# Eight recurrent heads: decay operands through PSUM, a reordered second turn, and a value tile in two column halves

## The reference, cut to what matters

```python
b = jnp.cumsum(logf, axis=2)
diff = b[:, :, :, None, :] - b[:, :, None, :, :]
decay = jnp.exp(jnp.minimum(diff, 0.0)) * causal
attn = jnp.einsum('bhtd,bhsd,bhtsd->bhts', q, k, decay)
o = (jnp.einsum('bhts,bhsv->bhtv', attn, v)
     + jnp.einsum('bhtd,bhdv->bhtv', q * jnp.exp(b), S))
b_last = b[:, :, -1:, :]
k_dec = k * jnp.exp(b_last - b)
S_new = (jnp.exp(b_last[:, :, 0, :])[..., None] * S
         + jnp.einsum('bhsd,bhsv->bhdv', k_dec, v))
```

## Time and profile before

| | |
|---|---|
| median of 3 runs | 852.73 us (850.11 to 853.77) |
| profiled execution | 853.36 us, its span 851.1 us |
| TensorE products busy | 811.1 us, 95% |
| VectorE / ScalarE / GpSimd busy | 405.9 / 233.0 / 141.5 us |
| head turns | about 21 to 170 us of the span |
| mean granted TensorE clock | 0.990 |

### The profile page before, as it was taken

One profiled execution on the slowest core, in us unless ns is written; L12 is line 12 of the kernel. 1 busy time (PEld: TensorE's weight loads), 2 busy tenths in 40 slices (PEclk: granted clock), 3 DMA queues, 4 the chain that ended last, 5 costly groups with the idle time before them and its releaser, 6 DMA issues.

```text
span 851.1 us, 12448 instructions
## 1 busy us (share of the span) xinstructions
PE 811.1 (95%) x5068; PEld 525.1 (62%) x5068; DVE 405.9 (48%) x682; ACT 233.0 (27%) x373; POOL 141.5 (17%) x170
## 2 busy tenths in 40 slices
PE   4999999999999999999999999999999999998892
PEld 2989999999999977585353533535335353352251
DVE  6789999988999723875011212112021120210127
ACT  6666655665444360111102010010000100000011
POOL 1354555433777200000000000000000000000000
PEclk9999999999999999999999999999999999999996
DMA  8422222344446453669999999999999999999971
GB/s 319 169 85 85 85 85 85 109 179 156 149 151 240 205 198 149 267 239 389 432 394 424 428 427 424 428 428 425 427 427 428 424 429 427 428 424 429 428 325 64
DMA packets 33894, 251.33 MB, mean 295 GB/s; under 512 B 4974, under 2 KB 8430, under 8 KB 21674
## 3 DMA queue, kind: packets, MB, share of 16 engines
q1 hardware_dynamic: 31296, 249.18, 71.8%
q10 hardware_dynamic: 2538, 1.32, 0.5%
HBM read 247.99 MB, written 2.48 MB: 294 GB/s over the span
## 4 chain that ended last, share of the span: by engine, by line
PE 69%; DVE 11%; DMA 9%; ACT 8%; issue 1%; ACTq 1%; DVEq 0%
PE ps L543 67%; DMA ring<-in_w_up_e 8%; DVE ring L1692 4%; ACT ring L1212 2%; ACT ar L1222 1%; DVE ar L1728 1%; ACT split_w L1131 1%; DVE ar L1739 1%; PE ps L940 1%; DVE ar L1683 1%; ACTq L1261 1%; ACT ar L1184 1%; DVE ring L1601 1%; DVE ar L1735 1%; ACT ar L1183 0%
## 5 line engine op out<-in xcount | busy, mean ns | idle before, releaser
L543 PE MATMUL ps<-ring,ar 128*64 128x512 f32 (+1 forms) x976 | 202.1, 567 | 1.6 <-DMA ring<-in_w_up_e 1.2
L543 PE MATMUL ps<-ring,xT 128*64 128x512 f32 (+2 forms) x848 | 151.0, 455 | 6.1 <-DMA ring<-in_w_gate_e 3.1
L543 PEld LDWEIGHTS ps<-ring,ar 128*64 128x64 f32 x976 | 67.9, 137 | 121.1 <-issue 111.8
L543 PEld LDWEIGHTS ps<-ring,xT 128*64 128x64 f32 (+1 forms) x848 | 75.5, 154 | 74.3 <-issue 63.8
L543 PE MATMUL ps<-split_x,split_t 128*128 128x320 f32 x672 | 99.2, 309 | 0.0
L543 PEld LDWEIGHTS ps<-split_x,split_t 128*128 128x128 f32 x672 | 98.6, 188 | 0.2
L2105 DVE TENSOR_TENSOR ar<-ar,ps 128x512 f32<-128x512 f32 (+1 forms) x42 | 28.7, 684 | 135.0 <-PE ps L543 134.3
L543 PE MATMUL ps<-split_x,split_w 128*128 128x320 f32 x480 | 79.8, 322 | 3.8 <-DVE split_w L1652 1.2
L543 PEld LDWEIGHTS ps<-split_x,split_w 128*128 128x128 f32 x480 | 73.2, 193 | 7.0 <-ACT split_x L1166 2.1
L1815 DVE SCALAR_TENSOR_TENSOR ps<-ar,params,ps 128x350 f32<-128x350 f32 x116 | 68.1, 587 | 4.1
L543 PE MATMUL ps<-ar 128*64 128x512 f32 (+7 forms) x424 | 66.8, 342 | 0.0
(11 more groups left out here) (232 smaller groups left out, 850.3 us busy)
## 6 DMA issues: line engine op xcount, KB each, us to landing
ring<-in_w_gate_e SPq DMA_DIRECT2D x29, 2048.0 KB, 21.8
ring<-in_w_up_e SPq DMA_DIRECT2D x29, 2048.0 KB, 18.6
ring<-in_w_down_e SPq DMA_DIRECT2D x22, 2048.0 KB, 18.1
ring<-in_w_in SPq DMA_DIRECT2D x56, 512.0 KB, 4.5
ar<-in_w_down_e SPq DMA_DIRECT2D x4, 1792.0 KB, 18.9
ring<-in_w_down_end SPq DMA_DIRECT2D x3, 2048.0 KB, 36.7
ar<-in_w_up_e SPq DMA_DIRECT2D x3, 1792.0 KB, 14.8
ring<-in_w_o_a SPq DMA_DIRECT2D x8, 512.0 KB, 5.8
```

The source lines that it names most:

```text
L543: return pe.matmul(out, lhsT, rhs, start=start, stop=stop)
```

## The change

- **VectorE's decays.** After the scan ScalarE's new `sum_copy` copies `hb` into PSUM bank 0 (signal `b_ps`). `level_decay` waits for it and takes its first operand there; the second, the broadcast end of the half, stays in SBUF. `cur_f` now waits for `dr_ready` (level_decay done).
- **Query sides.** `query_side` and the q product of `carry_side` read bank 1 instead of `hq`. The factor 128^-0.5 moves into the query weights (`w_high` and `w_low`). `cur_q` now waits for `qeb_ready` of the previous head.
- **Second turn.** On TensorE `levels` and `prev_kT` come ahead of `cur_q`. In the tail `levels(3, 1)` move ahead of the 16 small products into bank 1 and of `rms(3, 0)`.
- **V's third tile.** Its eight products alternate by k between output partitions 0 to 63 and 64 to 127, so that two partial sums arise. The key side of that tile is doubled to match (`hkde` has 384 columns, `levels` forms the third tile for both halves), and `prev_kT`, `prev_states` and `prev_out` use all 128 partitions, whose sum joins the two. The copies of V and kT on ScalarE become one instruction each; GpSimd's last add of `level_sums` becomes two.

```diff
             def cur_f(i, b, first):
-                    pe.wait_ge(h["ls_ready"], 2 * i + b)
+                    pe.wait_ge(h["dr_ready"], 2 * i + b)
             def cur_q(i, b, first):
-                    pe.wait_ge(h["q_sb"], 2 * i + b)
+                    pe.wait_ge(h["qeb_ready"], 2 * i + b)
             def value_tile(b, t):
                 for k in range(KT):
-                    last = mm(ps[0:n, 3, t * P:t * P + P], xT[:, k, t0:t0 + n], sh[:, b, 3, k, :], k == 0, k == KT - 1)
+                    if t < 2:
+                        last = mm(ps[0:n, 3, t * P:t * P + P], xT[:, k, t0:t0 + n], sh[:, b, 3, k, :], k == 0, k == KT - 1)
+                    else:
+                        side = slice(k % 2 * BLK, k % 2 * BLK + BLK)
+                        last = mm(ps[side, 3, t * P:t * P + P], xT[:, k, t0:t0 + n], sh[:, b, 3, k, :], k < 2, k >= KT - 2)
             def levels(i, b, first):
-                        for m in range(n // BLK):
-                            s0 = t0 + BLK * m
+                        for m in range(2):
+                            s0 = t0 + BLK * m * (t < 2)
             def prev_kT(i, b, first):
-                    last = pe.transpose(ps[0:n, 7, t * P:t * P + P], hkde[:, t0:t0 + n], ident)
+                    last = pe.transpose(ps[:, 7, t * P:t * P + P], hkde[:, t * P:t * P + P], ident)
             def prev_states(i, b):
-                    last = mm(ps[:, 7, t * P:t * P + P], hkT[0:n, t, :], hV[0:n, t, :], True, True)
+                    last = mm(ps[:, 7, t * P:t * P + P], hkT[:, t, :], hV[:, t, :], True, True)
             def prev_out(i, b, first):
-                mm(ps[:, 6, 256:320], hV[0:64, 2, :], hAS[0:64, 2, 0:64], False, True).then_inc(h["o_done"], 1)
+                mm(ps[:, 6, 256:320], hV[:, 2, :], hAS[:, 2, 0:BLK], False, True).then_inc(h["o_done"], 1)
             def head_turn(cur, prev, pprev, first=False, first_prev=False):
-                if first or first_prev:
+                if first:
                     cur_q(*cur, first)
                 if first_prev:
+                    levels(*prev, True)
                     prev_kT(*prev, True)
-                    levels(*prev, True)
+                    cur_q(*cur, first)
                     prev_states(*prev)
...
-            pe.wait_ge(h["ls_ready"], 8)
+            pe.wait_ge(h["dr_ready"], 8)
             conv_value(0)
-            pe.wait_ge(h["q_sb"], 8)
+            levels(3, 1, False)
+            pe.wait_ge(h["qeb_ready"], 8)
             for k in range(KT):
                 mm(ps[:, 1, T:T + 2 * NE], ones, wgb[:, k, :], k == 0, k == KT - 1)
             rms(3, 0, 1)
-            levels(3, 1, False)
             prev_kT(3, 1, False)
...
+            def sum_copy(i, b):
+
+                n = 2 * i + b
+                act.wait_ge(h["b_ready"], n + 1)
+                signal(act, act.activation(ps[:, 0, 0:T], hb, ACT.Copy), h["b_ps"], n + 1)
...
                 key_exp(*cur)
+                if first_prev:
+                    sum_copy(*cur)
                 if prev:
                     prev_states(*prev, first_prev)
+                if not first_prev:
+                    sum_copy(*cur)
...
             def level_sums(i, b, first):
-                signal(pool, pool.tensor_tensor(hAS[0:BLK, :, 0:BLK], hAM[0:BLK, :, 0:BLK], hAM[0:BLK, :, BLK:2 * BLK], ALU.add), h["as_ready"], 2 * n + 2)
+                signal(pool, pool.tensor_tensor(hAS[0:BLK, 0:2, 0:BLK], hAM[0:BLK, 0:2, 0:BLK], hAM[0:BLK, 0:2, BLK:2 * BLK], ALU.add), h["as_ready"], 2 * n + 1)
+                signal(pool, pool.tensor_tensor(hAS[:, 2, 0:BLK], hAM[:, 2, 0:BLK], hAM[:, 2, BLK:2 * BLK], ALU.add), h["as_ready"], 2 * n + 2)
...
             def level_decay(i, b):
+                dve.wait_ge(h["b_ps"], n + 1)
-                    ins = dve.tensor_tensor(xv[:, :, hs:2 * hs], bv[:, :, hs:2 * hs], bv[:, :, hs - 1:hs].to_broadcast([P, w // (2 * hs), hs]), ALU.subtract)
+                    here = ps[:, 0, 0:w].rearrange("p (m s) -> p m s", s=2 * hs)[:, :, hs:2 * hs]
+                    ins = dve.tensor_tensor(xv[:, :, hs:2 * hs], here, bv[:, :, hs - 1:hs].to_broadcast([P, w // (2 * hs), hs]), ALU.subtract)
             def query_side(i, b):
-                    qv = hq[:, b, 0:w].rearrange("p (m s) -> p m s", s=2 * hs)[:, :, hs:2 * hs]
-                    ins = dve.tensor_tensor(xv, xv, qv, ALU.mult)
+                    qv = ps[:, 1, 0:w].rearrange("p (m s) -> p m s", s=2 * hs)[:, :, hs:2 * hs]
+                    ins = dve.tensor_tensor(xv, qv, xv, ALU.mult)
             def carry_side(i, b, first):
-                signal(dve, dve.tensor_tensor(hqeb, heb, hq[:, b, :], ALU.mult), h["qeb_ready"], n + 1)
-                signal(dve, dve.tensor_tensor(hkde, hkde, hk[:, b, :], ALU.mult), h["kdec_ready"], n + 1)
+                signal(dve, dve.tensor_tensor(hqeb, ps[:, 1, 0:T], heb, ALU.mult), h["qeb_ready"], n + 1)
+                cc(dve.tensor_tensor(hkde[:, 0:SEQ], hkde[:, 0:SEQ], hk[:, b, 0:SEQ], ALU.mult))
+                both_sides = hkde[:, SEQ:SEQ + P].rearrange("p (s n) -> p s n", s=2)
+                key_twice = hk[:, b, SEQ:T].rearrange("p (o n) -> p o n", o=1).to_broadcast([P, 2, BLK])
+                signal(dve, dve.tensor_tensor(both_sides, both_sides, key_twice, ALU.mult), h["kdec_ready"], n + 1)
```

More of the change, by code:

```diff
@@ L630, in prev_kT @@
                     pe.wait_ge(h["so_ready"], 2 * i + b)
-                for t, (t0, n) in enumerate(TILES):
-                    last = pe.transpose(ps[0:n, 7, t * P:t * P + P], hkde[:, t0:t0 + n], ident)
+                for t in range(3):
+                    last = pe.transpose(ps[:, 7, t * P:t * P + P], hkde[:, t * P:t * P + P], ident)
                 last.then_inc(h["kT_done"], 1)
@@ L1130, in w_high @@
                     act.wait_ge(h[("f_done", "q_done")[q]], n)
-                signal(act, act.activation(piece(wh, q), sh[:, b, q].rearrange("p k n -> p (k n)"), ACT.Copy), whi_ready, 2 * n + q + 1)
+                signal(act, act.activation(piece(wh, q), sh[:, b, q].rearrange("p k n -> p (k n)"), ACT.Copy, scale=(1.0, QSCALE)[q]), whi_ready, 2 * n + q + 1)
             def u_high(c, q):
@@ L1221, in tile_exp @@
                 for t, (t0, c) in enumerate(TILES):
[L1222 to L1223 removed]
+                    dst, src = hkde[:, t0:t0 + c], hb[:, t0:t0 + c]
+                    if t == 2:
+                        dst = hkde[:, SEQ:SEQ + P].rearrange("p (s n) -> p s n", s=2)
+                        src = src.rearrange("p (o n) -> p o n", o=1).to_broadcast([P, 2, BLK])
+                    signal(act, act.activation(dst, src, ACT.Exp, scale=-1.0, bias=hb[:, t0 + c - 1:t0 + c]), h["kde_ready"], 3 * n + t + 1)
             def prev_states(i, b, first):
@@ L1651, in w_low @@
                 dve.wait_ge(whi_ready, 2 * n + q + 1)
-                signal(dve, dve.tensor_tensor(piece(wl, q), sh[:, b, q].rearrange("p k n -> p (k n)"), piece(whF, q), ALU.subtract), wlo_ready, 2 * n + q + 1)
+                raw = sh[:, b, q].rearrange("p k n -> p (k n)")
+                ins = dve.scalar_tensor_tensor(piece(wl, q), raw, QSCALE, piece(whF, q), ALU.mult, ALU.subtract) if q else dve.tensor_tensor(piece(wl, q), raw, piece(whF, q), ALU.subtract)
+                signal(dve, ins, wlo_ready, 2 * n + q + 1)
             def u_low(c, q):
@@ L1734, in last_mask @@
                     dve.wait_ge(h["as_ready"], 2 * n)
-                signal(dve, dve.tensor_tensor(hAM[0:BLK, 2, :], ps[0:BLK, LEVEL_BANKS[2], 0:LW], mask[0:BLK, :], ALU.mult), h["am_ready"], 2 * n + 2)
+                signal(dve, dve.tensor_tensor(hAM[:, 2, :], ps[:, LEVEL_BANKS[2], 0:LW], mask, ALU.mult), h["am_ready"], 2 * n + 2)
             def level_fold(i, b):
```

25 lines of the change are left out of this document (9 added, 16 removed).

## The result

The changed kernel takes 842.67 us (median of 5 runs, 841.39 to 844.99); the kernel before takes 850.81 (median of 5 runs: the three of the forecast's base and two more). The ratio is 0.9908 with a 95% interval of 0.9892 to 0.9923, that is 7.8 us off, where 5.8 were forecast. The predicted 847.0 and its range from 844.6 both lie above this, 1.9 us of it because the base itself went from 852.73 to 850.81. The direction and the circle that sets the new turn are as forecast; sizes were missed.

What follows compares the result with a forecast made beforehand. The start of TensorE's piece behind the eight head turns was taken to bound the kernel. -4.8 to rms of turn 7 and -0.8 after gave -5.6 (floor -6.3); -5.8 was taken: 847.0 us, range 844.6 to 851.0.

Steps and rivals of the forecast that it cites:

- rms of turn 2: TensorE after turn 1's new order and its hole: rms at 59.2 against 59.05, a loss of 0.15 us.
- What bounds the kernel: TensorE's piece from 181 to 367 us: its start moves its end, and the weight stream behind starts earlier by as much.
- The first circle: VectorE and ScalarE waiting on each other set the 19.24 us turn; with the change it becomes 17.6.
- level_decay: VectorE's seven instructions in a steady turn fall from 4.15 to 2.5 us with one operand in PSUM.
- sum_copy: ScalarE's new copy costs nothing in steady turns; in turn 0 level_decay starts 0.6 us later and ends 0.3 sooner.
- V's third tile: TensorE's eight products overlap in four pairs, saving 0.94 of V's 5.66 us a turn.
- K=128 instead of 64 does not change a product's columns: nothing: TensorE's third-tile products over 128 rows instead of 64 were priced at no change.
- the third circle: GpSimd's last add holds up prev_out; forget to prev_out 13.0, out, cur_f and 0.3 make an 18.27 us turn, 18.25 taken.
- TensorE's floor: TensorE's own work in a steady turn without waits: 19.06 less 0.94, 18.12 us.
- The tail: From rms of turn 7 to conv_gate(0): rstd's bare 1.7 us against rms no longer waiting 0.7; about even.
- rival 2: GpSimd's adds are both held up: turns of 18.6 us, +2, result 849; chance 0.10.
- rival 1: Turn 1's new 2.3 us hole drops TensorE's clock to half speed: +1.8 us, result 848.8; chance 0.14.

Runs made afterwards that it cites:

- K=128 products: The kernel before, with only the third tile's products of prev_states and prev_out run over all 128 partitions: 850.18 us, 0.9997.
- the filled hole: The changed kernel plus two unread products of 512 columns between cur_f(1) and levels(0) in TensorE's second turn: 842.71 us, 0.9883.
- w_low late: The changed kernel with prev_final moved ahead of w_low of the next head on VectorE: 839.72 us, 0.9864.
- the second set: Five more runs of the changed kernel, unchanged, against the kernel before: 841.72 us, 0.9877.

## Why the prediction was right and wrong

All comparisons are of profiled executions, the kernel before's against the changed one's, unless another is named.

| step | forecast | measured |
|---|---|---|
| rms of turn 2 | +0.15 | +1.28 (59.05 to 60.33) |
| five turns to rms of turn 7 | 5 x (18.25 - 19.24) = -4.95 | 89.43 - 96.21 = -6.78 |
| on to conv_gate(0) | -0.8 | -1.24 (25.49 to 24.25) |
| on to the end of TensorE's piece | 0 | -0.64 |
| sum | -5.6 (taken: -5.8) | -7.38 |

**What bounds the kernel: right.** The end follows the start of the piece behind the turns. From its end to the last product it is 468.4 us before, 467.5 after, and 464.4 to 468.4 in all fourteen profiles, which differ by 12 us in where the piece ends.

**The first circle: right.** Taking work off TensorE alone left the turn at 19.24 (K=128 products), and the whole change without level_decay's operand gave 19.02, of which the 0.22 are VectorE's and ScalarE's. Taking 1.7 us off VectorE alone gave 18.98, which is TensorE; I had taken 19.06 for that, where my own pieces add up to 19.04.

**level_decay: right.** 2.44 against 2.5, in the changed kernel and every variant that has the operand; the neighbour, not the columns, made it slow. sum_copy takes 0.44 as its nearest row, and no steady turn waits for it. In turn 0 I was wrong: level_decay waits 1.07 there, starts at 32.54 where it stood at 31.31, and its end is 0.3 later than before (35.02 against 34.70), not 0.3 sooner. w_low stands behind it and cur_f(1) behind w_low: 36.34 where 35.9 was forecast. As V(0) is shorter now, the hole ahead of cur_f(1) grew from 1.22 to 2.05.

**V's third tile: right.** 4.69 against 5.66 less 0.94.

**"K=128 instead of 64 does not change a product's columns: nothing": this step failed.** It looked at columns alone. A group with one product over 64 rows took 0.2 to 0.3 us longer than one without, 0.57 a turn on TensorE where the sum has 0. out lies on the third circle: 1.11 instead of 1.39, so 0.28 of the 0.35 by which the turn is shorter than 18.25 (0.20 by the experiment with K=128 alone). States lie on TensorE's floor: it came out at 17.45, not 18.12. The tail has states and out of two heads: in the piece behind conv_gate(0) states take 0.58 instead of 0.95 and out 1.03 instead of 1.29, 0.63 of its 0.64, and the head before gives a part of the 0.44. Over the turns this is 5 x 0.28 = 1.4 (1.0 by 0.20) of the 1.8 us by which the five turns beat the forecast. Whether it is the rows themselves or the change of tile between products stays open. The row was there to be read: the groups by shape show those products with a tile of their own and a longer mean.

**The third circle: right in kind, sized 0.35 too long.** The four terms come to 18.29 (18.27 was written, 18.25 taken); measured they are 0.20 + 12.99 + 1.11 + 3.60 = 17.90. forget starts 0.1 earlier than taken from turn 1. The add under w_low takes 1.18 where the tail's rows gave 1.32. The two terms of this error are out, 0.28, and forget, 0.10. Moving w_low away gave TensorE's floor, 17.45, so the circle is shown and not only argued. The sign that I had given for rival 2, a pause of over 0.3 us before prev_out, appeared (0.41) without the rival: the first add took 0.45 as before, and only the last one was held up. The sign could not tell the two apart.

**Turn 1: rival 1 happened in this profile, 1.54 us of it by the filled hole** (1.8 forecast). Without it rms of turn 2 would have come 0.26 earlier than before, where 0.15 later was forecast; with the query sides from SBUF, where the clock held, it came 0.17 earlier. Here too two pieces were forecast too long: states and out take 0.67 and about 1.14 in place of 0.96 and 1.39. My reason against the rival was one pause of 1.22 us that cost nothing. Of the pauses ahead of cur_f(1), those of 1.79 (w_low late), 1.87 and 1.97 were followed by 1.2 GHz, those of 1.71, 1.72, 2.05, 2.06 and 2.84 not; of those ahead of levels, 1.86 and 3.24 were, 1.78 and 1.82 not. So length alone doesn't decide it. I gave the rival 0.14 and thought of it as a property of the kernel; whether it strikes is one of the execution, and the hole ahead of cur_f(1), which the change widens, belongs to it as well.

**The tail: 0.44 better.** "About even" for rstd is what came, as conv_gate(0) waits only 0.52 for ScalarE; prev_out and the states there gained by K=128 too.

**The base.** 852.73 was the median of three runs; with two more it is 850.81, and beside the experiments 851.1 to 851.5. Of the 4.3 us between 847.0 and 842.67, 1.9 are the base and 2.4 the change. The range, 844.6 to 851.0, is 8.1 to 1.7 us below the base that it was made from. By medians the change is -8.1 us, by the ratio -7.8, so the change itself came out at the edge of the range, and that 842.67 lies 1.9 below it is the base's doing. In the profiles the piece's end moved by 7.38 where the sum had 5.6. That the total was not further off is in part luck: five turns (1.8), the tail (0.4) and the piece behind it (0.6) were better than forecast, and turn 1, by the clock, 1.1 worse. What follows the piece (some 7 us of the router at 1.2 GHz in the changed profile, none in the other; the 16 records at 807 us at half speed in the profile before only) differs by execution and does not belong to the change. That the second set of the changed kernel lies 1 us lower shows how little these runs tell below a us.

## What to carry to other kernels

List the circles of waits with their lengths before pricing anything: here the first two lay within 0.3 us, taking from either alone was worth 0 to 0.3 us a turn, and from both 1.34. Then list what the moved work lands on: a VectorE instruction with two SBUF operands that slid under a GpSimd one lengthened both (1.23 to 1.51 us, 0.32 to 1.18), and exchanging two calls repaired it. Read groups by shape for what sets a few instructions apart from their like before pricing their change at nothing.

## What the runs showed of the hardware

- One product over 64 of 128 rows made the group of states, three products, 0.29 us longer (0.96 against 0.67), at equal columns; out's group was 0.20 to 0.28 longer.
- Two products of 64 output columns each, in different column halves, took the time of one: the third tile's eight went in 0.9 us less than one after the other.
- A VectorE instruction with one operand in PSUM is not held up by GpSimd: seven in 2.44 us, against 4.06 to 4.15 with both in SBUF, whatever the stride of the PSUM operand (64 columns at a stretch down to single ones).
- Behind waits of 1.7 to 3.3 us TensorE was sometimes at 1.2 GHz (for some 3 to 7 us) and sometimes at full speed, with a wait of 2.84 among the latter, and in executions of the same kernel too. A long wait was not needed: in the profile with the query sides from SBUF the clock is at 0.50 from 173 to 176 us, behind some small products of 32 columns and a wait of 0.52, and conv_gate(0) takes 5.32 us; with the same wait of 0.52 it takes 3.79 in the changed kernel's profile. In the router, with products of 16 columns, the clock fell in 12 of 14 profiles.
